# A streaming-encoder trunk on one core: routing by halves of the tokens, one w2 kept aside, and the loop of eight experts written out

## What is computed

```
g_p, g_idx = top_k(softmax(xf @ wg + bg), 1)
e_in       = the 8 logits (xf @ we + be) of that group
top_v, top_i = top_k(e_in, 2);  gate = g_p * softmax(top_v)
y[token] += gate * ((silu(x @ w1[e]) * (x @ w3[e])) @ w2[e])   # for both experts e
```

## Time and profile before

| | |
|---|---|
| median of 3 runs | 1131.79 us (1131.2 to 1134.29) |
| profiled execution, its own time | 1131.81 us |
| its span in the profile | 1130.0 us |
| PE / DVE / ACT busy | 880.1 / 345.5 / 232.5 us |
| moved by DMA | 427.19 MB, mean 378 GB/s |
| chain that ended last, DMA ring<-in_moe_w | 43% |

### The profile page before, as it was taken

The page is one execution under the profiler, slowest core; times in us unless marked ns, Lnnn a source line. Parts: engine busy times, 40 slices in busy tenths (PEclk is TensorE's granted clock), DMA queues, the critical chain, the costliest instruction groups (busy, mean ns, idle before and its releaser), DMA issues.

```text
span 1130.0 us, 19738 instructions
## 1 busy us (share of the span) xinstructions
PE 880.1 (78%) x8032; PEld 511.3 (45%) x8033; DVE 345.5 (31%) x821; ACT 232.5 (21%) x559; POOL 4.6 (0%) x14
## 2 busy tenths in 40 slices
PE   6878777677786778589999988787887676768766
PEld 5644434333443344344886554443544343334433
DVE  2523222321322223222366253231332222213314
ACT  2421111110211111112144322110221121102112
POOL 1000000000000000000000000000000000000000
PEclk9899989998998989899999999999998898989979
DMA  9999999999999999998405459999999999999992
GB/s 299 428 424 424 425 426 425 423 427 425 426 425 426 425 426 426 425 425 358 176 1 200 166 208 426 425 426 413 426 426 425 425 426 425 428 423 425 427 426 112
DMA packets 33478, 427.19 MB, mean 378 GB/s; under 512 B 4706, under 2 KB 5986, under 8 KB 7988
## 3 DMA queue, kind: packets, MB, share of 16 engines
q1 hardware_dynamic: 33028, 424.19, 89.2%
q0 software_dynamic: 304, 0.72, 0.4%
HBM read 423.85 MB, written 1.05 MB: 376 GB/s over the span
## 4 chain that ended last, share of the span: by engine, by line
DMA 44%; PE 41%; DVE 7%; issue 5%; ACT 2%; DVEq 0%; SPq 0%
DMA ring<-in_moe_w 43%; PE ps L457 14%; PE ps L493 6%; PE ps L631 5%; PE ps L510 3%; PE ps L613 2%; DVE work L1061 2%; PE ps L411 2%; PE ps L685 2%; PE ps L363 1%; DMA work<-in_consts 1%; DVE work L1069 1%; ACT work L791 1%; PE ps L389 1%; DVE work L1063 1%
## 5 line engine op out<-in xcount | busy, mean ns | idle before, releaser
L457 PE MATMUL ps<-ring,work 128*32 128x256 f32 x4224 | 298.2, 434 | 164.8 <-DMA ring<-in_moe_w 100.7
L457 PEld LDWEIGHTS ps<-ring,work 128*32 128x32 f32 x4224 | 165.8, 124 | 304.7 <-issue 210.0
L1059 DVE TENSOR_SCALAR work<-work 128x128 f32<-128x128 f32 (+1 forms) x64 | 14.6, 229 | 501.3 <-ACT work L791 501.3
L493 PE MATMUL ps<-ring,work 128*32 128x256 f32 x2112 | 127.5, 382 | 30.8 <-DVE work L1069 30.2
L411 PE MATMUL ps<-work,h_sb 128*128 128x256 f32 (+1 forms) x576 | 136.2, 380 | 4.5 <-issue 3.8
L1095 DVE COPY hT<-ps 32x512 f32<-32x512 f32 x128 | 87.4, 683 | 149.0 <-PE ps L493 148.1
L791 ACT ACTIVATE work<-ps 128x256 f32<-128x256 f32 x64 | 24.5, 383 | 510.2 <-PE ps L457 510.2
L411 PEld LDWEIGHTS ps<-work,h_sb 128*128 128x128 f32 x576 | 99.6, 190 | 42.8 <-issue 32.9
L493 PEld LDWEIGHTS ps<-ring,work 128*32 128x32 f32 x2112 | 62.9, 109 | 92.9 <-DVE work L1069 44.9
L799 ACT COPY hT<-ps 32x512 f32<-32x512 f32 x128 | 73.9, 577 | 123.6 <-PE ps L493 122.9
L764 ACT ACTIVATE work<-ps,gcol 128x256 f32<-128x256 f32 (+1 forms) x144 | 58.6, 458 | 110.7 <-PE ps L411 110.7
(11 more groups left out here) (146 smaller groups left out, 420.8 us busy)
## 6 DMA issues: line engine op xcount, KB each, us to landing
ring<-in_moe_w SPq DMA_DIRECT2D x192, 2048.0 KB, 30.4
ring<-in_attn_wv SPq DMA_DIRECT2D x2, 2048.0 KB, 33.0
ring<-in_attn_wq SPq DMA_DIRECT2D x2, 2048.0 KB, 32.0
ring<-in_attn_wk SPq DMA_DIRECT2D x2, 2048.0 KB, 34.0
ring<-in_attn_wo SPq DMA_DIRECT2D x2, 2048.0 KB, 37.1
x_sb<-in_x SPq DMA_DIRECT2D x2, 512.0 KB, 5.7
work<-in_pool_w SPq DMA_DIRECT2D x1, 1024.0 KB, 13.0
out_x<-h_sb SPq DMA_DIRECT2D x2, 512.0 KB, 2.6
```

What stands on the lines that cost most here:

```text
L457: mm = pe.matmul(gu_ps[SB * j:SB * (j + 1), b, :, :], xg[:, u, kt, b, k, :], w[:, :, kt, P * j:P * (j + 1)], start=(kt == 0 and b == 0), s ...
L493: mm = pe.matmul(y_ps[SB * i:SB * (i + 1), b, :], actT[:, b, SB * j:SB * (j + 1)], w[:, j, 256 * i:256 * (i + 1)], start=(j == 0 and b == ...
```

## The change

There are four parts.

1. `GPB` becomes 8, so the 32 experts of a layer are written out and the `Fori` runs once, on PE, ACT and DVE; SP's loop is gone, and its waits are on constants.
2. In layer 1 the w2 of expert 0 (chunk 2) no longer goes into slot 2. Its halves go to `hT` and to words 2560 to 4607 of `work`, in two loads of 1 MB: one after the last head's attention product (`s_o`), one after the last logits (`s_lg`). Slot 2 takes chunk 10 (w3 of expert 3) instead, which therefore is not issued later. The chunk counts of slot 2 are one round ahead from there on.
3. Routing goes by halves. `choose`, `rank` and the gathering of the first group are done for tokens 0 to 127 as soon as their logits are there, and then for 128 to 255. The logits lie in banks 5 and 7, the first group is gathered into banks 0 to 3, and PE's `clear` products give way to one DVE `memset` of those banks before the loop. In layer 1 the second half's copy to `hT` is all DVE's.
4. In layer 1's order on PE, transposes, logits and ranks of half 0 go in between the heads of half 1's output projection.

The diff, cut to its core:

```diff
-GPB = 2
+GPB = 8
@@
-        sg = work[:, 4096:5120].rearrange("p (m b f) -> p m b f", m=4, b=NB)
+        sg = work[:, 4608:5632].rearrange("p (m b f) -> p m b f", m=4, b=NB)
...
+        aside = (hT.rearrange("p k s -> p (k s)"), work[:, 2560:4608])
@@
+        EARLY_C, ASIDE_C = RING + CPE - 1, CPE - 1
@@ SP
+            w2_aside = chunk_parts(1, 0, CPE - 1)
             for layer in range(2):
-                for c in range(RING):
+                for slot in range(RING):
+                    if layer == 1 and slot == RING - 2:
+                        sp.wait_ge(s_o, NH)
+                        sp.dma_start(aside[1], w2_aside[:, 2048:4096]).then_inc(s_aside, 16)
                     if layer == 1:
-                        sp.wait_ge(*attn_used[c])
-                    load(c, chunk_parts(layer, c // CPE, c % CPE), loaded[c])
+                        sp.wait_ge(*attn_used[slot])
+
+                    c = EARLY_C if layer == 1 and slot == ASIDE_C else slot
+                    load(slot, chunk_parts(layer, c // CPE, c % CPE), loaded[slot])
+                if layer == 1:
+                    sp.wait_ge(s_lg, 4)
+                    sp.dma_start(aside[0], w2_aside[:, 0:2048]).then_inc(s_aside, 16)
...
-                with sp.Fori(0, ITERS - 1) as it:
-                    for c in range(RING, RING + steady):
-                        stream(it, c)
                 for c in range(RING, steady):
-                    stream(ITERS - 1, c)
+                    if layer == 0 or c != EARLY_C:
+                        stream(ITERS - 1, c)
@@ PE
+            def logits_of(layer, number, t):
+
+                wait_hT(number, t)
+                for k in range(KT):
+                    mm = pe.matmul(ps[:, LOGITS[t], 0:NR], hT[:, k, t * P:(t + 1) * P],
+                                   wr[:, layer, k, :], start=(k == 0), stop=(k == KT - 1))
                 mm.then_inc(s_lg, 1)
-                for b in range(1, ACC):
-                    clear(b)
-                pe.wait_ge(s_A, layer + 1)
...
-                clear(0)
+            def ranks(layer, t):
+
+                pe.wait_ge(s_A, 2 * layer + t + 1)
+                if t > 0:
+                    pe.matmul(ps[:, RANKS[t], 0:NE], ones, A[:, 0, :], start=True, stop=False)
+                pe.matmul(ps[:, RANKS[t], 0:NE], upper, A[:, t, :], start=(t == 0), stop=True).then_inc(s_rk, 1)
...
+            def first_blocks(layer, t):
+
+                pe.wait_ge(s_hn, 2 * layer + t + 1)
+                if t == 0:
+                    pe.wait_ge(s_place0, layer + 1)
+                else:
+                    pe.wait_ge(main["onehot"], layer * (NGRP + 1) + 1)
                 for r in range(E4):
...
+            def other_blocks(layer):
+
+                pe.wait_ge(s_route, layer + 1)
                 most = pe.value_load(cnt[0:1, NE:NE + 1], min_val=0, max_val=S)
...
+                    if first and k == 0:
+                        pe.wait_ge(s_aside, 32)
+                        outputs(aside)
+                    else:
+                        from_ring()
@@ PE, layer 1
-                project(1, range(3, NH - 1))
+                project(1, range(3, 4))
                 transposes(2, 0)
+                project(1, range(4, 5))
+                logits_of(1, 2, 0)
+                project(1, range(5, NH - 1))
+                ranks(1, 0)
                 project(1, range(NH - 1, NH))
-
-                route(1, 2)
+                transposes(2, 1)
+                logits_of(1, 2, 1)
+                first_blocks(1, 0)
+                ranks(1, 1)
+                token_counts()
+                first_blocks(1, 1)
                 experts(1)
@@ DVE
+                ve.wait_ge(main["xgc"], (layer * (NGRP + 1) + 1) * E4)
+                then(ve.memset(ps[:, 0:4, :], 0.0))
@@ DVE, layer 1
             for t in range(TH):
                 residual(t, s_wo, 0)
-                copy_hT(2, t)
+                copy_hT(2, t, 1 - t)
                 token_factor(3, t)
-            route(1)
+                choose(1, t)
+                rank(1, t)
+            count_tokens(1)
             experts(1)
```

More of the change, by code:

```diff
@@ L188, in build @@
         s_out = sem("s_out")
+        s_aside = sem("s_aside")
         s_ssq = sem("s_ssq")
@@ L434, in first_blocks, with group @@
                     pe.wait_ge(s_xg1c[layer], E4)
-            def group(s, g, u, placed, rounds, fullest, tokens, chunk):
+            def group(s, g, u, placed, rounds, fullest, tokens, chunk, first=False):
                 def second_block(count, step):
@@ L593, in _ @@
             pe.wait_ge(s_c, 16)
-            route(0, 0)
+            pe.wait_ge(s_wr, 4)
+            for t in range(TH):
+                transposes(0, t)
+            for t in range(TH):
+                logits_of(0, 0, t)
+            for t in range(TH):
+                ranks(0, t)
+                if t == TH - 1:
+                    token_counts()
+                first_blocks(0, t)
             experts(0)
@@ L848, in _ @@
             act_e.wait_ge(gcol_in, 48)
-            for t in range(TH):
-                copy_hT(0, t)
-                norm(1, t, work[:, 0:D])
+            norm(1, 0, work[:, 0:D])
+            copy_hT(0, 0)
+            copy_hT(0, 1)
+            norm(1, 1, work[:, 0:D])
             for t in range(TH):
@@ L1153, in _ @@
             ve.wait_ge(gcol_in, 48)
-            for t in range(TH):
-                copy_hT(0, t)
-            for t in range(TH):
-                token_factor(1, t)
             ve.wait_ge(s_c, 16)
-            route(0)
+            copy_hT(0, 0)
+            token_factor(1, 0)
+            copy_hT(0, 1)
+            choose(0, 0)
+            token_factor(1, 1)
+            rank(0, 0)
+            choose(0, 1)
+            rank(0, 1)
+            count_tokens(0)
             experts(0)
```

163 lines of the change are left out of this document (79 added, 84 removed).

## The result

The changed kernel takes 1121.37 us in the median (1121.19 to 1121.57), beside 1131.76 for the kernel before in the same session: a ratio of 0.9901, 95% interval 0.9888 to 0.9914. The forecast was 1124.7 with a range of 1121.5 to 1128.5. The direction was right, and so were the two larger of the three costed gains; the third was too small, and two places costed at nothing gave something. The time lies 3.3 us under the forecast and 0.13 us under the range's low end. The profiled execution of after took 1121.49 us with a span of 1119.70, against 1131.81 and 1130.02, so the spans differ by 10.32.

The account below looks back on a forecast made before the run. Both expert layers were taken as bound by the weight stream, with T between: 1131.81 - 4.9 (w2) - 1.7 (routing) - 0.8 (loop) + 0.3 (fewer loads) = 1124.7 us, range 1121.5 to 1128.5.

Parts of the forecast that it names:

- T: Moment expert 0 of layer 1 finishes gate and up and the weight stream restarts; 667.8 us before, forecast 1.7 earlier.
- gate and up of expert 0: Layer 1's first expert products, ending at T: the same 3.65 us at full clock, up to 1.7 later at half clock.
- layer 0: Its routing, changed the same way, lies under a full weight stream with eight chunks queued: worth nothing.
- the loop written out: Expert loop without PE's returns: removes the thin stream at slice 28 in layer 1, 0.8 us, between 0 and 0.8.
- The w2 kept aside: Layer 1's expert 0 w2 moves in the trough, leaving 87 chunks after T instead of 88: gain 4.9 us.
- Routing in layer 1: Between attention and expert 0: 0.45 and 0.7 later, 1.3 and 1.6 earlier, making T about 1.7 us earlier.
- Fewer loads at the start: After T only two loads are queued, 9.8 us of data: 0.3 us lost, 1.5 at worst, 0 at best.
- The memset: DVE clears four banks before the loop, at most 2.8 us; expert 0's activation perhaps 0.4 us late, T unaffected.
- the first three: Rivals: routing gains nothing (24%), 1126.4; all works with full clock (15%), 1122.7; half 0 in the way (8%), 1129.3.
- the 15% case: Rival: all works, clock full at layer 1's logits, T 3.4 earlier, no hole: 1122.7, down to 1121.5 us; 15%.
- The fourth: Rival, straight code starves PE: written-out blocks stall PE in the expert layers; at 1.8 us each, 1143.9 us; 6%.
- The six returns: PE's loop-end branches, 6.02 us each in the median, mostly hidden behind weight waits; counting in full was a 2% rival.

Follow-up runs that it names:

- the padded one: Changed kernel with 64 zero products behind a never-taken branch, once per expert: 1244.22 us, ratio 1.1003.
- the two with an extra pass: Changed kernel with only first blocks of 32 tokens in the main path of both layers: 2150.57 us; the same with PE's gaps filled: 2152.93 us.
- the two pairs: Kernels without and with w2 aside, loop written out: old routing 1129.41 and 1123.94 us; routing by halves 1125.61 us and the changed kernel, 1121.37.
- first blocks alone in layer 0: Changed kernel whose layer 0 main path computes only first blocks of 32 tokens, the rest going to extra passes; layer 1 as changed: 1118.36 us, ratio 0.9870.
- its two variants: First blocks alone in layer 0 with PE's gaps around half 1's transposes filled: 1116.77 us; or with PE's later code shifted 96 instructions: 1118.59 us.
- the kernel with half the blocks: Apparently the changed kernel without the second 32-token blocks' code and branches (a little computation left out in layer 1): 1112.33 us, ratio 0.9817.

## Why the prediction came out as it did

The mechanism was right, weights in both layers with T between, and so were the two largest terms. What failed is the size of three others: gate and up of expert 0, put at nothing, gave 1.0 (1.2 with the issue behind it); layer 0, put at nothing, gave 0.4 on balance; the loop written out, 0.8, went with 1.4 in layer 1. The first of them is luck: shifts of the code take that stall away or bring it back. The rest that the total was over is within what two executions differ by.

- **What bounds the kernel: right.** Weights in both layers, T in between; each experiment but the padded one (and the two with an extra pass) moved the time through the stream, T or a layer's last expert.
- **The w2 kept aside, 4.9: right.** 4.9 and 5.2 in the two pairs. Both loads landed 1 to 1.5 us before I said, and no wait for them shows.
- **Routing in layer 1, 1.7: right in sum,** 1.6 in the trace, 1.3 to 1.8 in the pairs. Half 1's logits at 3.60 held (3.63), the residual's lag too (transposes at 646.05 for 646.17 before, where the whole stood 0.9 earlier, so 0.8 later and not 0.45). From logits to expert 0 it was 652.22 to 660.56, 8.3 us, against 3.5 + 4.85 reckoned: the choice took 0.4 more than that and the rest 0.4 less. The size of the gain is loose: from attention to gate and up, kernels with the new routing took 150.6 to 152.3 us and those with the old 153.2 to 153.9.
- **Gate and up of expert 0, "the same, 3.65": a stall taken for a fixed part.** The earlier trace rows gives 63 products of a group of 64. The last one, 0.62 us of issue later, stood in the next line, and the group took 4.68. My text even says "and a last piece, to 667.8" and then forecasts a change of nothing. With T's issue it is 1.17 us. I had weighed a loss of 1.7 here by the clock, and the clock was full. The kernel before has 3.66 when it is shifted, the changed one 4.68: no reasoning on the change could have got this term.
- **Layer 0, "worth nothing": a term left out.** It was true of routing. But the loop is written out in layer 0 too, and I costed that only in layer 1. It gave 0.9 us of stream in one pair of kernels and 1.4 in the other, and 1.2 between before and after. 0.7 was lost again behind it, by a stall of 1.31 in expert 30, so 0.44 are left. The first landing's 0.49 lies within what it differs by from kernel to kernel (23.0 to 25.0), with nothing changed ahead of it.
- **The loop written out, 0.8: the size too small, a second mechanism missed.** The hole in slice 28 went. But the stream of layer 1 got 1.4 us shorter in the pair with the old routing and 1.4 with the new. The fetches are what I missed: eight fewer after T, 1.4 us by the price of 0.18. That leaves next to nothing for the hole, and since the kernel before had the same 1.4 when it was merely shifted, only the sum is shown. I had used the 132 fetches of the earlier trace rows only as a threat to PE, and never asked what their 2.16 MB do to the DMA engines that I had just called the bound.
- **Fewer loads at the start, 0.3 lost: real, but not in the profiled execution.** There the third load came 8.2 us after T, inside the 9.8, the first slices after T run at 426, and the stream, 6.47 less, is 4.9 + 1.4 within 0.2. In the second trace of the same kernel it came at 9.6, with a loss of 0.7, and at 10.6 in *first blocks alone in layer 0*, whose stream took 1.2 to 1.5 us longer than that of its two variants.
- **The memset, at most 2.8:** 1.76 us, 661.16 to 662.92, so it ended before T, where 0.4 us of delay behind T were forecast.
- **The rivals.** None of the first three came; the clock at the logits stayed half, so the 15% case, which ends at 1121.5, is not what happened although its number is the nearest. The fourth is real and lies one block of jumped-over code per expert away. Its price was summed wrongly: by the earlier trace rows layer 0 leaves PE 121 us, 15.2 a group, so 14.4 would have cost nothing there, and of the 19 us only layer 1's half remained. The six returns were hidden, as I said against the rule: the whole worth of the loop was 2 to 3 us, not 36.
- **The range** held no term for where code comes to lie. Of three kernels shifted by 96 instructions two got slower, by 3 and 7 us, and one didn't move (0.2). The changed kernel shifted, at 1129.16 or by its ratio 1127.8, lies at the range's top as the unshifted one lies at its foot, by the same reasoning: where in the range the time fell, and that it fell out, was in part luck.

## What to carry to other kernels

In a kernel bound by its weight stream, count the instruction blocks that it fetches as bytes of that stream with a surcharge (16 KB at 425 GB/s would be 0.04 us, and cost 0.18), and look first at code that is jumped over: it is fetched, it isn't run, and the jump can stall the engine. Before believing a difference of a few microseconds between two kernels, shift the code of the engine that ends the chain by some idle instructions and look at it again; and cut both traces at the same events, which shows where a difference lies, with a second trace of one kernel to show what a stretch differs by on its own. Read a group of instructions to its last member, and ask of each number in a table of input sizes (here the tokens of an expert) whether the largest was seen.

## What the runs showed of the hardware

- A fetched block of 16 KB costs a DMA-bound stream 0.18 us (25 blocks fewer: 4.6 us in layer 1, 4.4 in layer 0), while it occupies one of 16 engines for 1.07. Eight of the 16 completions of a load come late, by 8.7 us in the median at the end of after's stream, and by 4.7 in the kernel with half the blocks.
- Skipping one more block of instructions per expert cost 122 us over 64 experts (1244.2 against 1121.4 to 1122.2 for the changed kernel): stalls of up to 6.1 us, and another engine at the bound. Inside a group of 64 products PE stopped on issue for over 0.5 us only in kernels that skip an If there: 13 times in the changed kernel, never in the one without these branches.
- A stall costs more than its length when the clock falls behind it: 3.60 us of nothing, then a gather of 3.78 instead of 1.99 (granted clock 0.5 from 501.7 to 508.5).
- The same 16 products of half 1's logits, behind the same gap of 1.38 us, took 3.63 us in one execution of the changed kernel, 2.61 in another, 2.22 and 1.97 in kernels that differ elsewhere. What decides on the clock there stays open.
- What stays open: why a stall comes at one skipped branch and not at the next. Its place moves with the code, its length (0.5 to 3.8 us inside a group of products, up to 6.1 with the padding) I could not derive.
